# Four homes instead of three for the gate weights of a mixture of experts, room taken from the dynamic DMAs' scratch

## The reference, cut to what matters

```python
h = jax.nn.silu(jnp.einsum("td,edf->tef", t, w_gate)) * jnp.einsum("td,edf->tef", t, w_up)
h = h * gates.astype(h.dtype)[..., None]
return jnp.einsum("tef,efd->td", h, w_down).reshape(B, L, D)
```

## Time and profile before

| | us |
|---|---|
| median of three runs | 634.96 |
| the profiled execution, own time | 635.95 |
| its span | 634.1 |
| PE busy | 566.3 |
| DVE busy | 247.6 |
| ACT busy | 142.4 |
| POOL busy | 62.9 |

### The profile page before, as it was taken

One profiled execution on the slowest core, in us unless ns is written; L12 is line 12 of the kernel. 1 busy time (PEld: TensorE's weight loads), 2 busy tenths in 40 slices (PEclk: granted clock), 3 DMA queues, 4 the chain that ended last, 5 costly groups with the idle time before them and its releaser, 6 DMA issues.

```text
span 634.1 us, 13240 instructions
## 1 busy us (share of the span) xinstructions
PE 566.3 (89%) x5748; PEld 380.8 (60%) x5748; DVE 247.6 (39%) x541; ACT 142.4 (22%) x271; POOL 62.9 (10%) x93
## 2 busy tenths in 40 slices
PE   1978999999999999959998988999999977888784
PEld 0565553466667556646446787998777754555341
DVE  2463267888863673472035870101111100111026
ACT  1051245423213760101015211100111000111022
POOL 2009300000001210002000110010001000000021
PEclk9988999999999999989999999999999999998898
DMA  8959933030330191499968979999999999999652
GB/s 259 392 206 376 368 109 132 0 133 20 115 128 5 39 395 41 153 376 353 247 232 341 404 253 333 395 407 398 421 416 425 422 417 422 424 426 428 265 198 99
DMA packets 50460, 173.94 MB, mean 274 GB/s; under 512 B 6401, under 2 KB 11520, under 8 KB 44000
## 3 DMA queue, kind: packets, MB, share of 16 engines
q1 hardware_dynamic: 36672, 149.08, 61.3%
q0 software_dynamic: 5520, 16.78, 7.1%
q10 hardware_dynamic: 8207, 7.21, 3.5%
HBM read 160.59 MB, written 12.46 MB: 273 GB/s over the span
## 4 chain that ended last, share of the span: by engine, by line
PE 33%; DMA 12%; DVE 6%; issue 2%; SPq 2%; ACT 0%; DVEq 0%
PE psum L942 12%; DMA slot<-in_w_down 5%; DMA slot<-in_w_gate 5%; PE psum L832 5%; PE psum L934 5%; PE psum L931 3%; DMA xe<-h_rows,lst 2%; PE psum L839 2%; PE psum L1087 1%; PE psum L848 1%; PE psum L492 1%; SPq L1235 1%; DVE SEL L2347 1%; PE psum L962 1%; DVE slot L2486 1%
## 5 line engine op out<-in xcount | busy, mean ns | idle before, releaser
L580 PE MATMUL psum<-hT,slot 128*128 128x384 f32 x304 | 100.8, 489 | 0.0
L580 PEld LDWEIGHTS psum<-hT,slot 128*128 128x128 f32 x304 | 56.9, 190 | 38.2
L942 PE MATMUL psum<-slot,xeTa 128*32 128x256 f32 x1152 | 67.5, 384 | 6.7 <-DMA slot<-in_w_gate 4.6
L942 PEld LDWEIGHTS psum<-slot,xeTa 128*32 128x32 f32 x1152 | 43.1, 111 | 30.2 <-issue 10.3
L589 PE MATMUL psum<-slot,hT 128*128 128x512 f32 x96 | 42.3, 595 | 1.1 <-DMA slot<-in_w_in 1.1
L1734 ACT ACTIVATE he<-psum 128x256 f32<-128x256 f32 (+1 forms) x16 | 6.6, 411 | 125.5 <-PE psum L942 97.1
L2426 DVE TENSOR_TENSOR he<-he,psum 128x256 f32<-128x256 f32 (+1 forms) x16 | 7.3, 455 | 68.2 <-PE psum L942 50.7
L2444 DVE COPY ye<-psum 128x256 f32<-128x256 f32 (+1 forms) x15 | 6.9, 461 | 68.9 <-PE psum L942 43.7
L2430 DVE COPY heT<-psum 128x256 f32<-128x256 f32 (+1 forms) x16 | 7.3, 458 | 66.0 <-PE psum L962 66.0
L942 PE MATMUL psum<-slot,heT 128*32 128x256 f32 x512 | 31.1, 394 | 2.2 <-DMA slot<-in_w_down 1.1
L934 PE MATMUL psum<-slot,xeTa 128*32 128x128 f32 x288 | 32.7, 273 | 0.0
(11 more groups left out here) (487 smaller groups left out, 934.8 us busy)
## 6 DMA issues: line engine op xcount, KB each, us to landing
slot<-in_w_ada SPq DMA_DIRECT2D x12, 2048.0 KB, 13.3
slot<-in_w_gate SPq DMA_DIRECT2D x12, 2048.0 KB, 18.8
slot<-in_w_up SPq DMA_DIRECT2D x12, 2048.0 KB, 21.6
slot<-in_w_down SPq DMA_DIRECT2D x11, 2048.0 KB, 18.0
slot<-in_w_in SPq DMA_DIRECT2D x7, 2048.0 KB, 9.1
const<-in_w_gate SPq DMA_DIRECT2D x4, 1792.0 KB, 14.4
y_rows<-T POOLq DMA_DIRECT2D x11, 384.0 KB, 15.7
slot<-in_w_out SPq DMA_DIRECT2D x2, 2048.0 KB, 17.1
```

The costliest lines, as they stand in the source:

```text
L580: last = mm(o[:, 0:TOK], w[:, kt, tile(i)], hT[:, kt, :], start=(kt == 0), stop=(kt == KT - 1))
L942: last = mm(psum[32 * c:32 * c + 32, bank, 0:HALF], x(k, c % 2), w(k)[:, c // 2 * HALF:c // 2 * HALF + HALF], start=(k == 0), stop=(k == t ...
```

## The change

Gate weights get a fourth home, `fourth_gate`, of 16 KB a partition. The scratch of the dynamic DMAs is set to 2048 bytes a partition. Up and down keep three homes. `of_set` now has a kind: for gate, position n uses home n % 4 up to 11, and 0, 1, 3, 0 for 12 to 15. Gate 3 goes to the new home and waits for nothing but `perm`. It is issued before the wait for `sel_used`. The loads' order becomes gate 3, the piece of position 2's down, gate 4; then for each n: up n, gate n + 2, down n.

```diff
-        def of_set(n):
+        def of_set(n, k=1):
+            if k == 0:
+                return n % 4 if n < 12 else (0, 1, 3, 0)[n - 12]
             return n % 3 if n < 12 else n % 2
 
-        def use(n):
-            return sum(of_set(m) == of_set(n) for m in range(n))
-
-        def user_before(n):
-            return max(m for m in range(n) if of_set(m) == of_set(n))
+        def use(n, k=1):
+            return sum(of_set(m, k) == of_set(n, k) for m in range(n))
+
+        def user_before(n, k):
+            return max(m for m in range(n) if of_set(m, k) == of_set(n, k))
...
+        fourth_gate = eb("fourth_gate", [P, KT, CW])
...
-                if of_set(n) == 2:
+                if of_set(n, k) == 3:
+                    pe.wait_ge(s["fourth_gate"], 16 * (use(n, k) + 1))
+                    return rows_of(fourth_gate)
+                if of_set(n, k) == 2:
...
-            sp.wait_ge(s["sel_used"], NT)
-            third_down_c(2)
...
-                sp.wait_ge(s[("gate_done", "up_done", "down_done")[k]], user_before(n) + 1)
-                if of_set(n) < 2:
-                    load_expert(e, of_set(n), k, 0, n=n)
+                if (n, k) != (3, 0):
+                    sp.wait_ge(s[("gate_done", "up_done", "down_done")[k]], user_before(n, k) + 1)
+                if of_set(n, k) == 3:
+                    sp.dma_start(fourth_gate[:, :, :], source(e, 0)).then_inc(s["fourth_gate"], 16)
+                elif of_set(n, k) < 2:
+                    load_expert(e, of_set(n, k), k, 0, n=n)
...
             sp.wait_ge(s["perm"], 1)
             reload(3, 0)
+            sp.wait_ge(s["sel_used"], NT)
+            third_down_c(2)
+            reload(4, 0)
             for n in range(3, E):
                 reload(n, 1)
-                if n + 1 < E:
-                    reload(n + 1, 0)
+                if n + 2 < E:
+                    reload(n + 2, 0)
                 if n < E - 1:
                     reload(n, 2)
...
-    nc = bacc.Bacc("TRN2", target_bir_lowering=False, num_devices=1)
+    nc = bacc.Bacc("TRN2", target_bir_lowering=False, num_devices=1, dynamic_dma_scratch_size=2048)
```

More of the change, by code:

```diff
@@ L388, in backbone_step @@
             "pool_step", "qd", "res_in", "rg_a", "rg_b", "rg_b2", "rgo", "ro_ready",
-            "rope", "route", "rs_ready", "rtail", "sel", "sel_used", "lists", "perm", "third_gate", "third_up", "third_down", "siluc",
+            "rope", "route", "rs_ready", "rtail", "sel", "sel_used", "lists", "perm", "third_gate", "fourth_gate", "third_up", "third_down", "siluc",
             "sp_abs", "sp_in", "c_in", "filt1_in", "filt2_in", "win_in", "veca_in", "vecb_in", "ret_in", "bada_in", "zeroed",
@@ L992, in weights @@
             def weights(n, k):
-                if of_set(n) == 2:
+                if of_set(n, k) == 3:
+                    pe.wait_ge(s["fourth_gate"], 16 * (use(n, k) + 1))
+                    return rows_of(fourth_gate)
+                if of_set(n, k) == 2:
                     name, count = (("third_gate", 32), ("third_up", 48), ("third_down", 80))[k]
-                    pe.wait_ge(s[name], count * (use(n) + 1))
+                    pe.wait_ge(s[name], count * (use(n, k) + 1))
                     return (third_gate, third_up, third_down)[k]
-                p = of_set(n)
-                pe.wait_ge(loaded[home(p, k)], 16 * (use(n) + 1 + (PRE_USES if p else 0)))
+                p = of_set(n, k)
+                pe.wait_ge(loaded[home(p, k)], 16 * (use(n, k) + 1 + (PRE_USES if p else 0)))
                 return halves_of(slot[home(p, k)]) if k == 2 else rows_of(slot[home(p, k)])
@@ L1062, in down_by_pieces @@
                         name, count = (("third_gate", 32), ("third_up", 48), ("third_down", 80))[k - 1]
-                        pe.wait_ge(s[name], count * (use(11) + 1) + 16)
+                        pe.wait_ge(s[name], count * (use(*((10, 0) if k == 1 else (11, 1))) + 1) + 16)
                     for half in range(2):
@@ L1306, in _ @@
             e = sp.value_load(perm[0:1, E - 1:E], min_val=0, max_val=E - 1)
-            sp.wait_ge(s["down_done"], user_before(E - 1) + 1)
+            sp.wait_ge(s["down_done"], user_before(E - 1, 2) + 1)
             for k in range(FE // P):
```

## The result

The kernel with the change takes 636.15 us (median of 20 runs, 633.15 to 640.84); the kernel before, run beside it on the same chip, takes 633.0 us (20 runs, 629.68 to 636.83). The ratio is 1.005, 95% interval [1.0028, 1.0072]: about 3.2 us slower. The time lies 0.35 us from the predicted 635.8, but the difference is +3.2 us, not the +0.8 of the sum. So the closeness is luck: two errors cancel, because the kernel before was faster here than in the three runs that the prediction started from. What needs an explanation is some 2.4 us that the sum did not have.

A forecast was written before the change was run, and what follows sets the result against it. It took the landing of down 13's weights from full DMAs, plus a tail, to bound the kernel. Gate 3 and order 0, waits 0, gather +0.8, scratch 0 on 634.96 gave 635.8 us; range 631.8 to 638.1.

The forecast's parts named there:

- What bounds the kernel: End of program: set by the landing of down 13's weights, plus a tail that no weight DMA bounds.
- Gate 3 earlier, with the new order: Expert weight stream: 4.96 us of DMA work done early, paid back by one more gate tile ahead; sum 0.
- The gather: Position 1's gather beside gate 3: landing after 7.1 to 12.3 us, costing 0 to +1.6 us; middle +0.8 taken.
- The +1.6: Upper end for position 1's gather: 12.3 us landing, PE 4.3 us late, less 2.66 us of later idle time.
- Waits and counts: PE's semaphore waits: as many as before, one landing instead of two in three places; 0 us.
- scratch: POOL's dynamic DMAs: smaller scratch costs 0 us, as 116 us of cover would hide an early stall.
- Behind down 13: Last loads: one tile less there, so down 15 lands about 5 us sooner, behind PE's own work; nothing gained.
- Rival 2: At `load_x(1)`: position 1's gather takes 16.0 us and stops PE, the stream issued 5.3 us later; 640.3 us, chance 0.14.
- Rival 1: Weight stream: head start reaches the end, rate rising from 412 to 423 GB/s; -4.5 us, 630.5 us, chance 0.17.
- Rivals 3 and 4: Scratch too small for POOL, lengthening issues, chance 0.03; early gate 3 issue on SP not taking effect, no change, 0.01.

The follow-up runs named there:

- order_back: Kernel with the change, but gates loaded two positions ahead only until n = 7 and in the old order from n = 9; ratio to the kernel before 0.9986.
- after_again: The kernel with the change, unchanged, measured and traced a second time; ratio to the kernel before 1.0015.
- back_at_13: Kernel with the change, with only gate 15 put back in its old place behind down 13 and up 14; ratio to the kernel before 1.0015.
- scratch_only: Kernel before with the dynamic DMAs' scratch set to 2048 bytes and nothing else; ratio to the kernel before 0.998.
- before_again: The kernel before, unchanged, measured and traced a second time; ratio 0.999.
- gate3_late: Kernel with the change, but gate 3 issued behind the wait for `sel_used`; four homes and new order stay; ratio to the kernel before 1.0053.
- turn_silu: Kernel with the change, position 1's transposes behind up 0 on PE and gate 0's silu ahead of their copy on ACT; ratio to the kernel before 0.9966.
- turn_later: Kernel with the change, with position 1's transposes on PE moved from ahead of up 0 to behind it; ratio to the kernel before 1.0042.
- before_turn_later: Kernel before, with position 1's transposes on PE moved behind up 0 and nothing else; ratio to the kernel before 1.0027.

## Why the prediction was right or wrong

**What bounds the kernel: right.** The measured ratios rise and fall nearly as down 13 does, and down 13 follows the stream, but for the three traces named above. Down 13 itself started at 572.42, 2.4 us ahead of 574.78 where 2 were allowed; counted from `perm` it is 1.7 us later, and only that count tells of the change.

**Gate 3 earlier, with the new order (sum 0): this step failed.** Half of it held: one more tile ahead costs about its own length, 5.2 us by the landings in after and order_back. The other half, that 2.1 MB more would have landed, did not. Against the mean of the three traces with the old order after had only 57.84 - 57.31 = 0.53 MB more, 1.3 us instead of 4.96. That leaves 3.7 us by the account, 2.9 by the traces (213.1, the mean of after and after_again, less 210.2), beside 3.2 us in the timed runs. The step took the idle time of the DMAs for room that a tile can have for nothing. But the loads behind it are issued on PE's counts, and a PE that comes later issues them later: down 3 went out 33.8 us behind `perm` instead of 30.7. The third window gave back (403 - 379) x 43 us = 1.0 MB (403 is the mean of those three traces), while the hole that was to close moved to 34 us behind `perm` (share 0.47).

**The gather (+0.8): mis-sized.** It took 11.8 us, near the upper bound of 12.3, and 11.6 again in after_again and in back_at_13; 7.1 or 7.2 in the traces that issue gate 3 late. Two terms were missing in its price. PE's idle time of 3.72 us was followed by the lower clock: 0.50 and 0.67 in the two windows behind it, a triple of products of gate 1 taking 0.87 us there against 0.50 later. And the 2.66 us of idle time before position 2 that was to absorb most of it is no constant: it is 2.66 in before, 0.95 in scratch_only and none in before_again, where that gather landed in 9.7 us instead of 12.3. Position 1's hidden transposes come at +43.7 and +43.5 us behind `perm` in after and after_again, against +40.9, +38.6 and +39.6 in the three traces with the old order. The Trainium skill (DMA: Bandwidth & Descriptors, Queues, rings and completion order) has each DMA engine take turns between queues with work. The trace of after agrees: the gather issued beside gate 3 alone (11.8; a piece of down 2 and gate 4 joined only for its last 5.1 and 3.5 us) and the one beside more weights (11.7) cost the same. The +1.6 that it gave was the better choice of the two.

**Waits and counts, scratch: right, the second for a narrower reason.** The 7.1 us of gate waits went and moved to up and down (10.1 us, expected some 11). The scratch does stall POOL, and only the cover makes it free.

**Behind down 13: right.** The four last weight pieces are issued from 577.69 on and take 12.1 us to landing in the median; counted from the first issue that is 17.4 us behind down 13's start, and before it was 22.3. That is the 5 us forecast, and nothing came of it.

**The rivals.** Rival 2 named the right place and half of the mechanism, but at 11.8 us of landing it would have cost 1.1 us by its own rule; gate3_late shows that the loss stands without it. Rival 1's price was real but not of this change: 423 GB/s before down 13 were there already, and it takes turn_silu's PE to raise the window ahead of that. Rivals 3 and 4 did not occur.

**What stays open.** The span behind down 13 goes from 55.9 to 63.7 us between traces, and from 59.3 to 63.7 between two of the same kernel. It varies by more than the effect studied here. (The 55.9 belongs to turn_silu, whose trace has an own time of 626.12 us, 5.6 below its median.) Clock, the length of a stretch of "issue" on PE and a late multiplication on DVE differ there; none was tried alone.

## What to carry to other kernels

Where the DMAs are the bound, a tile that is asked for earlier stands ahead of every other tile: price it as a loss of its own length for all of them, and book the gain only as bytes that have really landed more when the DMA-bound stage begins. Prefetch deeper while the compute engine sets the pace, and return to the order of need before the DMAs set it. Before idle DMA time is filled, look at what small transfer was living in it, and at what the engine behind that transfer issues.

## What the hardware showed that was not expected

- A gather of 96 rows landed in 7.1 to 7.2 us where the DMAs moved 207 to 221 GB/s in the 10.5 us behind `perm`, and in 11.6 to 11.8 us where one more weight tile was under way (365 GB/s and more). Those of the next position took 9.7 to 12.3.
- An idle time of 3.72 us on PE was followed by a granted clock of 0.50 over 2 us and 0.67 over the next 2; in turn_later the 2.70 us end at 378.88, and the clock is 0.56 from 378 to 380 and 0.59 from 380 to 382. In gate3_late, without such idle time ahead of gate 1, the window from 373.64 to 396.14 shows 1.00. The length of the idle time alone doesn't decide: in before 2.66 us end at 387.73 and the clock from 387.48 to 389.48 is 1.00, and gate 14 took 3.66 us behind 2.40 us in before_turn_later but 5.20 behind 2.43 in order_back.
- With 2048 bytes a partition of scratch and nothing else changed, POOL stood for 15.08 us among its early DMAs, and the time of the kernel did not change (0.998).
